# Seven block products in place of eight in six pieces' down projection, with weight sums formed by adding DMAs and operand sums on VectorE

## The reference, cut to what matters

```
D_MODEL = 1024; D_FF = 4096; SEQ = 512; DN_ALPHA = 4 ** 0.25
def _sq_relu_mlp(h, w1, w2):
    return jnp.square(jax.nn.relu(h @ w1)) @ w2
x = _layernorm(DN_ALPHA * x + g2 * _sq_relu_mlp(x * (1.0 + s2) + sh2, ffn_w1[i], ffn_w2[i]), ln2_g[i], ln2_b[i])
```

## Time and profile before

| | us |
|---|---|
| median of three runs | 2003.45 |
| span of the profiled execution (first to last instruction) | 2001.8 |
| what lies around the span (median less span) | 1.65 |
| TensorE busy | 1991.0 |
| VectorE busy | 1197.8 |
| ScalarE busy | 602.0 |
| GpSimd busy | 483.5 |
| the six loop pieces (relu of up0 in the first to that in `ffn1z`, 1695.40 to 1956.93) | 261.53 |

### The profile page before, as it was taken

The page is one execution under the profiler, slowest core; times in us unless marked ns, Lnnn a source line. Parts: engine busy times, 40 slices in busy tenths (PEclk is TensorE's granted clock), DMA queues, the critical chain, the costliest instruction groups (busy, mean ns, idle before and its releaser), DMA issues.

```text
span 2001.8 us, 26691 instructions
## 1 busy us (share of the span) xinstructions
PE 1991.0 (99%) x9765; PEld 1710.1 (85%) x9765; DVE 1197.8 (60%) x1683; ACT 602.0 (30%) x861; POOL 483.5 (24%) x366
## 2 busy tenths in 40 slices
PE   9999999999999999999999999999999999999998
PEld 6889889889988998898888888888888888888887
DVE  4756678787655755566764553644553586544547
ACT  3423122244212221222424223223323343332223
POOL 0300321334331135233350010020020036322323
PEclk9999999999999999999999999999999999999999
DMA  9623334323433432344322132122222232333332
GB/s 342 232 64 82 119 114 130 105 85 116 142 95 110 126 110 89 113 129 138 105 69 63 52 98 67 53 90 63 74 64 79 64 105 74 102 98 95 115 105 74
DMA packets 76420, 207.56 MB, mean 104 GB/s; under 512 B 13232, under 2 KB 26160, under 8 KB 76208
## 3 DMA queue, kind: packets, MB, share of 16 engines
q1 hardware_dynamic: 74512, 202.57, 33.0%
q10 hardware_dynamic: 1824, 3.85, 0.6%
HBM read 204.26 MB, written 2.12 MB: 103 GB/s over the span
## 4 chain that ended last, share of the span: by engine, by line
PE 97%; DMA 1%; DVE 0%; POOL 0%; issue 0%; ACT 0%; SPq 0%; POOLq 0%; ACTq 0%; DVEq 0%
PE bank L760 24%; PE bank L762 24%; PE bank L761 24%; PE bank L798 7%; PE bank L800 7%; PE bank L799 7%; PE bank L1064 1%; PE bank L1113 1%; PE bank L976 1%; DMA mod<-mod_units_d 0%; PE bank L948 0%; PE bank L998 0%; PE bank L999 0%; PE bank L996 0%; PE bank L1199 0%; DMA raw<-w_units_d 0%
## 5 line engine op out<-in xcount | busy, mean ns | idle before, releaser
L1683 DVE TENSOR_TENSOR w_lo<-raw,w_hi 128x1024 fp32r<-128x1024 f32 x234 | 312.6, 1336 | 366.5 <-ACT w_hi L1341 366.2
L1341 ACT ACTIVATE w_hi<-raw 128x1024 fp32r<-128x1024 f32 x234 | 246.8, 1055 | 661.2 <-PE bank L762 451.8
L2356 POOL TENSOR_TENSOR res_lat<-res_lat,gy 128x512 f32<-128x512 f32 x160 | 221.6, 1420 | 697.8 <-DVE gy L1792 589.5
L760 PE MATMUL bank<-hT_hi,w_hi 128*128 128x384 f32 (+2 forms) x1088 | 379.5, 349 | 0.0
L762 PE MATMUL bank<-hT_hi,w_lo 128*128 128x384 f32 (+2 forms) x1088 | 377.9, 347 | 0.0
L761 PE MATMUL bank<-hT_lo,w_hi 128*128 128x384 f32 (+2 forms) x1088 | 377.9, 347 | 0.0
L798 PE MATMUL bank<-w_hi,hT_hi 128*128 128x512 f32 x592 | 230.6, 389 | 0.0
L799 PE MATMUL bank<-w_lo,hT_hi 128*128 128x512 f32 x592 | 230.3, 389 | 0.0
L800 PE MATMUL bank<-w_hi,hT_lo 128*128 128x512 f32 x592 | 230.3, 389 | 0.0
L760 PEld LDWEIGHTS bank<-hT_hi,w_hi 128*128 128x128 f32 x1088 | 204.5, 188 | 13.5 <-DVE w_lo L1683 0.7
L761 PEld LDWEIGHTS bank<-hT_lo,w_hi 128*128 128x128 f32 x1088 | 204.5, 188 | 12.8 <-issue 0.2
(11 more groups left out here) (275 smaller groups left out, 3010.4 us busy)
## 6 DMA issues: line engine op xcount, KB each, us to landing
raw<-w_units_d SPq DMA_DIRECT2D x255, 512.0 KB, 3.6
mod1a<-mod_units_d SPq DMA_DIRECT2D x32, 384.0 KB, 3.9
mod1b<-mod_units_d SPq DMA_DIRECT2D x32, 384.0 KB, 4.2
bv<-mod_units_d SPq DMA_DIRECT2D x16, 512.0 KB, 3.9
mod<-mod_units_d SPq DMA_DIRECT2D x14, 512.0 KB, 7.7
mod<-mod_units_d SPq DMA_DIRECT2D x19, 256.0 KB, 6.1
vtok<-mod_units_d SPq DMA_DIRECT2D x8, 512.0 KB, 3.9
lnbc<-ln_d SPq DMA_DIRECT2D x8, 512.0 KB, 5.1
```

The costliest lines, as they stand in the source:

```text
L760: nc.tensor.matmul(out, s_hi, m_hi, start=first, stop=False)
L1341: nc.scalar.activation(halves_of(phase, k, i)[0], raw[:, s, :], ACT.Copy).then_inc(hi_done, 1)
L1683: tt(lo, raw[:, s, :], f32(hi), ALU.subtract).then_inc(lo_done, 1)
L2356: gt(r, r, gy[:, e % 2, :], ALU.add).then_inc(res_added, 1)
```

## The change

In the six loop pieces the down projection is a product of a 2 by 2 arrangement of blocks: the activations A (512 hidden features by 512 tokens) in four blocks of 256 by 256, the down weights B in the four units B11, B12, B21, B22 (256 features by 512 outputs each). It is formed by seven block products, with sums of blocks on both sides. Each product is 2 token tiles by 2 feature blocks by 3 matmuls, 12 matmuls of 512 columns, 84 in all. The products go straight into sums over the pieces (`acc`, five accumulators in SBUF, without gate), and the gate is multiplied in once, at the end. The hardware loop is written out. `PRODUCTS` lists number, first bank, and whether the bank is opened afresh (otherwise the product goes on top of the one before it in that bank).

```diff
+PRODUCTS = [(1, 0, True), (7, 4, True), (2, 0, False), (4, 4, False), (5, 2, True), (6, 0, True), (3, 2, False)]
+_STRASSEN = [(f"up{c}.0", (6, 7, 2, 3)[c], "D") for c in range(CH)]
+_STRASSEN += [(f"q{q}.{t}", b + t, "D") for q, b, _ in PRODUCTS for t in range(2)]
-    ("ffn1", PIECES_F - 2, _FFN1 + _down(LAT, 4), dict(units=8, stage=CH, full=CH, add=2 * LAT)),
+    ("ffn1", PIECES_F - 2, _STRASSEN, dict(units=8, splits=CH + NPROD, stage=NPROD)),
+        BLOCK_RAW = {CH: B11, CH + 2: B21, CH + 6: B22}
+        BLOCK_SUM = {CH + 1: T3, CH + 3: T4, CH + 4: T1, CH + 5: T2}
+        T_BASE = {T3: B12, T1: B11, T2: B22, T4: B21}
+        a11, a21 = stage[:, :, 0:256], stage[:, :, 256:512]
+        a12, a22 = gy[:, :, 0:256], gy[:, :, 256:512]
+        OPERANDS = [a11, s_of[S3], a12, a22, s_of[S1], s_of[S2], s_of[S4]]
 sync:
+            sp.wait_ge(pe_step, step_of("ffn1a", 0, "up3.0"))
+            for x in (T3, T1, T2, T4):
+                load_base(0, x)
+            for p in range(PIECES_F - 2):
+                ...
+                for x in range(4):
+                    sp.wait_ge(lo_done, split + x + 1)
+                    load(at + 9 if x == B12 else at + CH + UNIT_OF[x], x)
+                sp.wait_ge(lo_done, split + CH + 1)
+                load(at + 8, B11)
+                if p < PIECES_F - 3:
+                    load_base(p + 1, T3)
+                sp.wait_ge(lo_done, split + CH + 3)
+                load(at + 11, B21)
+                if p < PIECES_F - 3:
+                    for x in (T4, T1, T2):
+                        load_base(p + 1, x)
+                sp.wait_ge(lo_done, split + CH + NPROD)
+                load(at + 10, B22)
 tensor:
+            def strassen(p):
+                for c in range(CH):
+                    feature_unit("ffn1", p, c, [(f"up{c}.0", 0, TOKL)])
+                for n, (q, b, opens) in enumerate(PRODUCTS):
+                    pe.wait_ge(lo_done, before("splits", "ffn1", p) + CH + n + 1)
+                    pe.wait_ge(stage_lo, count("stage", "ffn1", p, n))
+                    ...
+                    for t in range(2):
+                        free("ffn1", p, f"q{q}.{t}")
+                        ...
+                        for kk in range(2):
+                            ...
+                            nc.tensor.matmul(out, a_hi[:, kk, tt], hi[:, w], start=opens and kk == 0, stop=False,
+                                             skip_group_check=True)
+                            ...
 scalar, per piece:
+                block_hi(p, 2); block_hi(p, 3); relu(0); block_hi(p, 4); relu(1); block_hi(p, 5)
+                operand_hi(p, 0); operand_hi(p, 1); relu(2); block_hi(p, 6); relu(3); block_hi(p, 7)
+                for n in (2, 3, 4): operand_hi(p, n)
+                block_hi(p, 8); operand_hi(p, 5); block_hi(p, 9); operand_hi(p, 6); block_hi(p, 10)
+                block_hi(p + 1, 0); block_hi(p + 1, 1)
 vector, per piece (accumulate: acc = acc +- bank, two tiles each):
+                block_lo(p, 2); block_lo(p, 3); square(0); block_lo(p, 4); square(1)
+                operand_sum(S3); operand_lo(0); block_lo(p, 5); operand_lo(1)
+                square(2); block_lo(p, 6); square(3)
+                operand_sum(S1); operand_lo(2); operand_sum(S2); operand_lo(3); block_lo(p, 7)
+                operand_sum(S4); accumulate(1); operand_lo(4); block_lo(p, 8); accumulate(7)
+                operand_lo(5); block_lo(p, 9); accumulate(2); operand_lo(6); block_lo(p, 10)
+                accumulate(4); accumulate(5); block_lo(p + 1, 0); accumulate(6); block_lo(p + 1, 1); accumulate(3)
 vector, last piece (the wait for folded[t] is in drain_add, ahead of each addition of a bank to the residual):
+            combine([(C12, ALU.subtract)])              # acc -= SUM16, 128x1024
             ffn("ffn1z", ...)
+                        if c in (1, 2):
+                            gate_sum(*((C11, 0, 0), (C12, 1, 1))[c - 1])
+            combine([(C21, ALU.add), (Z57, ALU.subtract)])
+            gate_sum(C21, 0, 2)
+            gate_sum(Z57, 1, 3)
             final_blocks("ffn1z")
+                    dve.wait_ge(folded[t], 16)
 gpsimd:
+            def weight_sum(p, x):
+                pool.wait_ge(t_base[x], 16 * (p + 1))
+                if x == T2:
+                    pool.wait_ge(t_sum[T1], 16 * (p + 1))
+                if x == T4:
+                    pool.wait_ge(t_sum[T2], 16 * (p + 1))
+                other = (w_units[at + UNIT_OF[B22]], w_units[at + UNIT_OF[B12]], wsum[:, T1, :], wsum[:, T2, :])[x]
+                nc.gpsimd.dma_start(wsum[:, x, :], other, accum_op=ALU.add).then_inc(t_sum[x], 16)
-            ln_shift(before("add", "ffn1"), lnbc1, LAT)
-            with nc.gpsimd.Fori(0, PIECES_F - 2) as p:
-                add("ffn1", p, LAT)
+            nc.gpsimd.memset(acc[:, :, :, :], 0.0).then_inc(acc_zero, 1)
+            for p in range(PIECES_F - 2):
+                for x in (T3, T1, T2, T4):
+                    weight_sum(p, x)
+                if p == 0:
+                    ln_shift(before("add", "ffn1"), lnbc1, LAT)
+            for t in range(LAT):
+                pool.wait_ge(fold_mul, 2 if t < 2 else 4)
+                part = acc[:, 0:2, t, :] if t < 2 else acc[:, 2:4, t - 2, :]
+                nc.gpsimd.dma_start(res(t)..., part, accum_op=ALU.add).then_inc(folded[t], 16)
```

More of the change, by code:

```diff
@@ L203 @@
     PER[_n].update(_k)
+    PER[_n].setdefault("splits", PER[_n]["units"])
 BASE = {}
@@ L246, in implied @@
 def implied(phase, label):
-    if phase.startswith("ffn0") and label in ("up0.0", "up0.1"):
+    if phase.startswith("ffn0") and label in ("up0.0", "up0.1") or phase == "ffn1" and label in ("up2.0", "up3.0"):
         return False
@@ L398, in build @@
         mod1_in = [sem(f"mod1_in{s}") for s in range(SLOTS_M1)]
+        t_base = [sem(f"t_base{x}") for x in range(4)]
+        t_sum = [sem(f"t_sum{x}") for x in range(4)]
+        s_sum = sem("s_sum")
+        relu_done = sem("relu_done")
+        acc_zero = sem("acc_zero")
+        combined = sem("combined")
+        fold_mul = sem("fold_mul")
+        folded = [sem(f"folded{t}") for t in range(LAT)]
         const_in = sem("const_in")
@@ L788, in token_units @@
                     k = k0 + q
-                    pe.wait_ge(lo_done, before("units", phase, i) + (k + 1))
+                    pe.wait_ge(lo_done, before("splits", phase, i) + (k + 1))
                     hi, lo = halves_of(phase, k)
@@ L872, in part @@
                         seen.add(k)
-                        pe.wait_ge(lo_done, before("units", phase) + (k + 1))
+                        pe.wait_ge(lo_done, before("splits", phase) + (k + 1))
                     hi, lo = halves_of(phase, k)
@@ L989, in part @@
                     if pair == 0 and not low:
-                        pe.wait_ge(lo_done, before("units", phase) + k + 1)
+                        pe.wait_ge(lo_done, before("splits", phase) + k + 1)
                         free(phase, 0, label)
@@ L1285, in part @@
                             seen.add(k)
-                            pe.wait_ge(lo_done, before("units", "ffn1z") + (k + 1))
+                            pe.wait_ge(lo_done, before("splits", "ffn1z") + (k + 1))
                         hi, lo = halves_of("ffn1z", k)
@@ L1638, in _ @@
             ffn("ffn1a", 0, 1, TOKL, act_hi1)
-            with nc.scalar.Fori(0, PIECES_F - 2) as p:
-                ffn("ffn1", p, 1, TOKL, act_hi1)
+            for p in range(PIECES_F - 2):
+                strassen(p)
             ffn("ffn1z", 0, 1, TOKL, act_hi1)
@@ L1679, in split_lo @@
                     return
[L1680 removed]
+                dve.wait_ge(hi_done, count("splits", phase, i, k))
                 s, _ = unit_in(phase, i, k)
```

240 lines of the change are left out of this document (218 added, 22 removed).

## The result

| | median us | range, runs | span of the profiled run |
|---|---|---|---|
| before | 2003.47 | 2003.44 to 2003.55, 4 | 2001.8 |
| after | 2014.07 | 2013.1 to 2015.64, 4 | 2011.3 |

The ratio is 1.0053, interval 1.0041 to 1.0066: slower by half a per cent. The prediction said 2002.35, with a range of 1994 to 2012; the result lies 2 us above it.

What follows compares the result with a forecast made beforehand. TensorE was taken to bound the kernel, busy 1991.0 of 2001.8 us. Terms -16.3 - 0.5 + 8.7 + 5.1 + 1.9 = -1.1 gave a span of 2000.7, a median of 2002.35, range 1994 to 2012.

Steps and rivals of the forecast that it cites:

- What goes: Loop pieces: 12 matmuls fewer each, 16.3 us in six, plus 0.49 of stalls; 40.80 us a piece without a wait.
- What comes on VectorE: Queue between up3 and the first accumulation holds TensorE: 1.45 us of each piece come back, 8.7 in six.
- The adding DMAs: Weight sums T1, T2, T4 run one behind another; 5.2 us each to landing, hidden in steady pieces.
- X: An adding DMA's time from issue to landing, put at 5.2 us, bounds 3.5 and 10.9.
- rival 2: Adding DMAs bound through the chain T1, T2, T4: 2009 us at X = 8, 2029 at 10.9; chance 0.14.
- The first of six pieces, `ln_shift`: First loop piece: T4 late by 1.9 us, GpSimd additions slow VectorE by 3.2; together 5.1, bounds 3 and 9.
- Rival 3: VectorE a little slower throughout, from accumulations or GpSimd's DMA issue: 1 us a piece, 2008 us; chance 0.13.
- The end: Combining and gating accumulators: `final_blocks` starts 3.5 us late, 1.9 later at the end, fold hidden; bounds 0 and 3.5.
- the upper bound of 9: First loop piece: most it could lose, 9 us, if all eight `ln_shift` additions met VectorE operations.

Runs made afterwards that it cites:

- e3: Kernel after with only VectorE's order changed: three accumulations moved ahead of operations not yet needed, S4 moved back; 2004.67 us, ratio 1.0006.
- f4: Kernel after with first sums issued early, VectorE reordered, `ln_shift` as adding DMAs, and the end relieved; 1987.99 us, ratio 0.9921.
- g1: Kernel before plus one tiny GpSimd DMA right ahead of `ln_shift`, into an existing unused tile so addresses stay; 2012.44 us, ratio 1.0042.
- e4: Kernel after plus one short VectorE addition into a spare tile ahead of `accumulate(1)` in each of six pieces; 2017.68 us, ratio 1.0074.
- f1: Kernel after with first sums issued early and each `ln_shift` addition waiting on a semaphore for the one before; 2003.58 us, ratio 1.0001.

## Why the prediction was wrong

The sum was -1.1 for the span; it was +9.5. Of the 10.6 between them 9.1 lie in the first piece, 0.5 in the other five, 0.9 at the end. Step by step:

- **What goes**: right. e3 and f4 show the 40.80 of a piece without a wait.
- **What comes on VectorE**: right, down to the queue. `accumulate(1)` was put at t = 5.85 and began at 1773.86 - 1768.01 = 5.85; product 2 at 6.70 and began at 6.67. The 0.2 ahead of product 4 is there too: its first two matmuls come 0.36 and 0.31 us apart (1777.26, 1777.62, 1777.93) where 0.227 is usual. 42.35 for 42.25; 0.5 us in five pieces.
- **The adding DMAs**: this is the first step that failed. X = 5.2 was a load's 3.6 plus its data once more; measured, the median is 6.7 to 6.9 (4.5 to 9.9), and the sums come in a chain. How much of it is the adding, the issuing engine, or the traffic beside it stays open. T1, issued within a microsecond of T3, took 10 us; T2 took 7.5. T4 went out at 1716.08 and not at 1708.8, and landed at 1720.6 and not at 1714.0. The rival had the rule ready ("each us of X above 4.3 puts T4 back by 3"; by the prediction's own 1.9 us for X = 5.2 it should read 4.6), and I gave it 14 in a hundred, though no row showed a DMA of this kind: the value lay near the lower bound, 3.5, by an argument on bytes alone. `operand_lo 2` began at t = 1722.26 - 1711.60 = 10.7 instead of 4.2: 6.5 us. In steady pieces the DMAs were hidden, as said. The prediction's estimate from the Trainium skill, "DMA: Bandwidth & Descriptors", section "Anatomy of one DMA — SWDGE (gpsimd) path", 3.2 us, was further off than mine.
- **The first of six pieces, `ln_shift`**: the second that failed, in its mechanism. I let the additions cost 1.06 to 1.08 for each VectorE operation that met one, as in the earlier trace rows, three times, 3.2 us. In fact one operation met all that were left, 5.05 for 0.69, 4.4 us, as VectorE is shut out when a GpSimd DMA issue stands ahead of the additions (g1). Why the issue does this stays open. Rival 3 had named "GpSimd's DMA issue holding it up as its additions do", but as a small steady cost; the issues themselves hold up nothing in steady pieces.
- **The clock**: left out. The 13.8 us of idle time that the two made together were followed by eight matmuls at the 1.2 GHz level, 1.6 us. 6.5 (late T4) + 1.2 (additions, 4.4 for 3.2) + 1.6 = 9.3, against 56.41 - 47.35 = 9.1.
- **The end**: `final_blocks`' first addition came 3.3 us later against up3's end (3.5 said). At the end 2.8 were left, not 1.9. What the trace shows in the way: the fold's four DMAs of 256 rows go out one at a time, 5.4 to 5.5 us apart (the third also waited for VectorE's gating, which ended at 1988.2), so the first reciprocal root, on the same queue, ran only at 1994.75, and ScalarE and VectorE waited for it:

```profile
1988.13 0.69 DVE L2155 TENSOR_TENSOR res_lat<-bank,res_lat 128x512 f32<-128x512 f32 x1
...
1994.01 1.21 POOL L2777 DMA_DIRECT2D res_lat<-acc  x1 [4.16 <-issue]
1994.75 1.06 POOL L2635 TENSOR_TENSOR rstd<-veps,tiny 128x1 f32<-128x1 f32 x1
1995.93 1.16 ACT L1830 ACTIVATE res_lat<-res_lat,rstd 128x1024 f32<-128x1024 f32 x1 [12.98 <-POOL rstd L2635]
...
2000.73 1.41 DVE L2176 SCALAR_TENSOR_TENSOR res_lat<-res_lat,mv,bank 128x512 f32<-128x512 f32 x2 [0.90 <-ACT bank L1824]
```

I had called the fold hidden by looking at its landing alone, and not at what is queued behind its issue. No run moves the fold by itself, so the 0.9 is read from this chain and not shown by an edit. The range failed with the first piece: the upper bound of 9 took all eight additions with a T4 that was 1.9 late at most, rival 2 took the late T4 with the additions cheap, and nothing took both with the clock on top. That piece holds 56.41 - 40.80 = 15.6 us of waits and slow matmuls, where its bound let it hold about 10.5.

## What to carry to other kernels

Before a chain of dependent DMAs is called hidden, price its first round by itself: in the second piece T4 went out some 18 us before it was wanted and cost nothing, in the first it went out 4 us after, and landed 8.3 us late. Where a product accumulates on top of another, the operation that empties the bank should not stand behind work that nobody needs yet; four moves in VectorE's order were worth 1.55 us a piece (e3). And an experiment that adds a tile changes addresses too: put the tile last (as in e4, where the matmuls kept their 389 ns) or into a gap (g1), and run the tile without the rest beside it.

## What the runs showed of the hardware that I had not expected

- Eight unwaited GpSimd additions (128x512, both inputs in SBUF) right behind a DMA issued by GpSimd run in 9.9 to 10.4 us and hold a VectorE operation with two SBUF inputs until they are over (5.05, 5.07, 5.07, 8.53, 8.68, 11.23, 11.56 us). Without the issue, or with a semaphore wait between the additions (f1), they take 12.8 to 13.9 us and VectorE is 1.1 to 1.7 late at a time. Why the issue changes this was not found; that it does was shown by adding it alone.
- Tiles 32 bytes further in SBUF made matmuls of 512 columns 3% slower (0.2333 for 0.2267 us) where one operand lay in them and the other in a tile that had not moved, and not where both had moved; 17.5 us in the kernel.
- An adding DMA of 512 KB issued by GpSimd takes 6.7 to 6.9 us to landing where a plain load issued by SyncE takes 3.4, from SBUF and from DRAM alike (kernel after).
- GpSimd issued adding DMAs of 256 rows (two runs a partition) only 5.4 to 5.5 us apart, and what stood behind them in its queue waited.
